# Rotation doublings by group, sample operands earlier, U copies dealt out, and output rows turned inside the last layer

## The reference

```python
h = modulate(rmsnorm(x, norm_pre[0]), sh0, sc0)
x = x + 0.5 * gt0 * rmsnorm(swiglu(h, ffn1_in, ffn1_out), norm_post[0])
h = modulate(rmsnorm(x, norm_pre[1]), sh1, sc1)
u, q, k, v, q_idx, k_idx, w_idx, gate_a, gate_b = jnp.split(h @ w_in, splits, axis=-1)
y_ssm, s_re, s_im = s5_mixer(u, h0_re, h0_im, ...)          # 32 groups of 16 channels, 64 complex states each
y_a = (y_ssm @ glu_w) * jax.nn.sigmoid(y_ssm @ glu_v)
attn = attention_fn(q, k, v, q_idx, k_idx, w_idx)           # indexer scores, top-k keys, softmax
mixed = (sigmoid(gate_a) * y_a + sigmoid(gate_b) * (attn @ w_branch_attn)) @ w_out
x = x + gt1 * rmsnorm(mixed, norm_post[1])
x = x + 0.5 * gt2 * rmsnorm(swiglu(modulate(rmsnorm(x, norm_pre[2]), sh2, sc2), ffn2_in, ffn2_out), norm_post[2])
```

## Time and profile before

| | |
|---|---|
| median of 3 runs | 3160.18 us (3159.11 to 3163.3) |
| the profiled execution, device time | 3145.66 us |
| its span (first to last instruction or transfer) | 3143.9 us |
| mean granted TensorE clock | 0.955 |
| busy: PE, DVE, ACT, POOL | 93%, 54%, 38%, 12% |
| last x block ready, first turn of the last block | 3131.74, 3132.66 us |

### The profile page before, as it was taken

How to read it: one execution, slowest core, us unless ns; L and a number is a source line. 1 busy time by engine, 2 the same in 40 slices (tenths; PEclk the granted TensorE clock), 3 DMA queues, 4 the chain that set the end, 5 groups by cost and what they waited for, 6 DMA issues and landing times. The chain is left out here.

```text
span 3143.9 us, 55982 instructions
## 1 busy us (share of the span) xinstructions
PE 2910.3 (93%) x21922; PEld 2715.4 (86%) x21922; DVE 1691.9 (54%) x3314; ACT 1191.6 (38%) x2019; POOL 379.2 (12%) x430
## 2 busy tenths in 40 slices
PE   6899999889999989999869999997999889999997
PEld 5899999789776689999848999997997766999997
DVE  5442346877768474223364424478777684732234
ACT  5532333445344243222254323344453432522221
POOL 2100000214015100000021000011240340100000
PEclk8999999899999999999979999989999999999998
DMA  7443442312123333232174434323221243232321
GB/s 241 133 150 107 135 145 78 125 48 62 48 78 109 103 105 87 77 98 83 51 234 128 147 105 145 124 77 125 55 61 50 76 128 103 83 97 84 104 73 62
DMA packets 452487, 324.09 MB, mean 103 GB/s; under 512 B 25113, under 2 KB 403345, under 8 KB 451546
## 3 DMA queue, kind: packets, MB, share of 16 engines
q1 hardware_dynamic: 446906, 296.60, 31.4%
q0 software_dynamic: 5408, 25.17, 2.4%
HBM read 310.48 MB, written 11.24 MB: 102 GB/s over the span
## 5 line engine op out<-in xcount | busy, mean ns | idle before, releaser
L1187 PE MATMUL PS<-h_hi,w_hi 128*128 128x260 f32 (+1 forms) x4000 | 840.6, 292 | 42.1 <-POOL h_lo L2678 28.3
L1187 PE MATMUL PS<-h_lo,w_hi 128*128 128x260 f32 (+1 forms) x4000 | 816.1, 286 | 0.0
L1781 DVE TENSOR_TENSOR lo_apart<-stage,w_hi 128x1024 fp32r<-128x1024 f32 (+2 forms) x448 | 498.5, 1147 | 432.8 <-ACT w_hi L779 425.8
L1187 PEld LDWEIGHTS PS<-h_hi,w_hi 128*128 128x128 f32 (+1 forms) x4000 | 629.6, 192 | 91.6 <-issue 72.9
L1187 PEld LDWEIGHTS PS<-h_lo,w_hi 128*128 128x128 f32 (+1 forms) x4000 | 627.4, 192 | 0.0
L779 ACT ACTIVATE w_hi<-stage 128x1024 fp32r<-128x1024 f32 (+3 forms) x586 | 541.8, 954 | 76.3 <-DMA stage<-in_mod_w 40.0
L1187 PE MATMUL PS<-h_hi,lo_apart 128*128 128x260 f32 x2816 | 570.3, 285 | 0.0
L1187 PEld LDWEIGHTS PS<-h_hi,lo_apart 128*128 128x128 f32 x2816 | 437.8, 190 | 0.0
L1925 DVE TENSOR_TENSOR hidf<-sil,PS 128x520 f32<-128x520 f32 x88 | 61.3, 696 | 420.9 <-PE PS L1187 420.9
L1187 PE MATMUL PS<-hid_lo,w_hi 128*128 128x260 f32 x1408 | 285.3, 284 | 0.0
L1187 PE MATMUL PS<-hid_hi,w_hi 128*128 128x260 f32 x1408 | 284.5, 283 | 0.0
(11 more groups left out here) (428 smaller groups left out, 4055.7 us busy)
## 6 DMA issues: line engine op xcount, KB each, us to landing
stage<-in_ffn_in SPq DMA_DIRECT2D x176, 512.0 KB, 3.8
stage<-in_mod_w SPq DMA_DIRECT2D x144, 512.0 KB, 4.7
stage<-in_w_in SPq DMA_DIRECT2D x72, 512.0 KB, 3.6
stage<-in_ffn_out SPq DMA_DIRECT2D x64, 384.0 KB, 3.3
stage<-in_ffn_out SPq DMA_DIRECT2D x64, 320.0 KB, 3.1
stage<-in_w_out SPq DMA_DIRECT2D x16, 512.0 KB, 3.5
x_hold<-xT SPq DMA_DIRECT2D x2, 2080.0 KB, 6.5
xT<-x_hold SPq DMA_DIRECT2D x2, 2080.0 KB, 8.2
```

The lines of the kernel that those rows point to most:

```text
L1187: return nc.tensor.matmul(out, lhsT, rhs, start=start, stop=stop)
L1781: nc.vector.tensor_tensor(lows(ch)[:, ch.slot, 0:ch.elems], stage[:, ch.slot, 0:ch.elems], w_hi[:, ch.slot, 0:ch.elems].bitcast(FP32), ALU ...
```

## The change

VectorE: all doublings leave the qi loop. Doublings 0 and 1 come after it, doubling 2 after `new_keys` in u tile 0, 3 and 4 behind score groups 1 and 3. The last two doublings are made for four pairs at a time (`last_rotations(t)`), for t = 0 before gate tile 0, for t + 1 behind `skipped(t)`. `samples_operands` stands ahead of the split of u1. The clears of BX and BXl go to GpSimd, ahead of its wait for the powers; VectorE waits for `bx_zeroed`.
ScalarE: the copies of u tile u-1 are made in quarters between the key copies of tile u; those of tile 3 stay behind it.
The end: in the last layer, TensorE turns each x block to rows as soon as it is stepped (three row tiles; the fourth for blocks 4 to 7, its blocks 0 to 3 last, because its bank holds the roots), the samples after block 2. ScalarE and VectorE copy half rows, SyncE sends each row tile when both halves are there. The rows lie over `h_hi` and `h_lo`. The block after the layers goes.

```diff
-    def chunked_inputs(u, pair):
-
-        for q in range(4):
+    def chunked_inputs(u, pair, q):
...
                 for u in range(4):
                     split(chunk('u', u + 2))
                     if u == 1:
                         keys_turned(0)
-                    for g in scored_beside(u):
+                    for n, g in enumerate(scored_beside(u)):
                         if g + 1 < PAGE // 8:
                             keys_turned(g + 1)
-                    act.wait_ge(chunk_used, chunk('u', u).number(1))
-                    for dst, src in chunked_inputs(u, (u + 1) % 2):
-                        nc.scalar.activation(dst, src, ACT.Copy)
-                    nc.scalar.activation(us[:, u, :], PS[:, (u + 1) % 2, 1, HALF - DEC:HALF], ACT.Copy).then_inc(ev_a, 1)
+                        if n < 4:
+                            inputs_by_chunk(u - 1, n)
+                for q in range(4):
+                    inputs_by_chunk(3, q)
...
+                def rows_turned_out():
+                    for k in range(KD):
+                        pe.wait_ge(x_ready, 2 * KD + k + 1)
+                        if k == 2:
+                            pe.wait_ge(xs_stepped, 3)
+                            for f in range(KD):
+                                last = turn(PS[0:DEC, 2 + f // 4, 1, f % 4 * P:(f % 4 + 1) * P], xT[:, f, T:TOK], P)
+                            last.then_inc(x_turned, 1)
+                        if k == 4:
+                            pe.wait_ge(x_copied, 1)
+                        for t in range(TT if k >= 4 else TT - 1):
+                            last = turned_row(t, k)
+                            if k == KD - 1:
+                                last.then_inc(x_turned, 1)
+                        if k == 3:
+                            last.then_inc(x_turned, 1)
+                    for k in range(4):
+                        last = turned_row(TT - 1, k)
+                    last.then_inc(x_turned, 1)
...
+                def last_rotations(t):
+                    at = slice(4 * t, 4 * t + 4)
+                    for q in (levels - 2, levels - 1):
+                        n = 1 << q
+                        x1, x2 = etmp[:, 0, :, 0:n], etmp[:, 1, :, 0:n]
+                        for r, op in enumerate((ALU.subtract, ALU.add)):
+                            cn, sn = (pw[:, 2 + q, z, at].unsqueeze(2).to_broadcast([P, 4, n]) for z in (r, 1 - r))
+                            own(nc.vector.tensor_tensor(x1, E[:, 0, at, 0:n], cn, ALU.mult))
+                            tt(x2, E[:, 1, at, 0:n], sn, ALU.mult)
+                            tt(E[:, r, at, n:2 * n], x1, x2, op)
...
                     if u == 2:
                         poles()
-                        dve.wait_ge(x_spilled, 16)
-                        own(nc.vector.memset(E[:, 0, :, 0:1], 1.0))
-                        own.step(nc.vector.memset(E[:, 1, :, 0:1], 0.0))
-                        rotations(0, 2)
-                    if u == 3:
-                        rotations(2, 5)
-                split(chunk('ki', 2))
+                dve.wait_ge(x_spilled, 16)
+                own(nc.vector.memset(E[:, 0, :, 0:1], 1.0))
+                own.step(nc.vector.memset(E[:, 1, :, 0:1], 0.0))
+                rotations(0, 2)

                 for u in range(4):
-                    split(chunk('u', u + 2))
                     if u == 0:
                         dve.wait_ge(ev_a, evicts_a['ki'] + 1)
                         samples_operands()
-                        rotations(5, 6)
+                        split(chunk('ki', 2))
                         new_keys()
+                        rotations(2, 3)
+                    split(chunk('u', u + 2))
                     for g in scored_beside(u):
                         weighted(g)
-                        if g in (0, 2):
-                            last_rotation(g // 2)
+                        if g in (1, 3):
+                            rotations(3 + g // 2, 4 + g // 2)
                         if g == 5:
                             held_inputs()
                         if g == 7:
-                            dve.wait_ge(h0_ready, 1)
-                            own(nc.vector.memset(BXl[:], 0.0))
-                            own.step(nc.vector.memset(BX[:], 0.0))
+                            dve.wait_ge(bx_zeroed, 1)
                             plain_inputs(0)
...
                 counted(0.0)
+                last_rotations(0)
...
                     if g % 4 == 3:
                         skipped(t)
+                    if g % 4 == 3 and t < 3:
+                        last_rotations(t + 1)
...
+                def half_row(t):
+                    nc.vector.tensor_copy(yrow[:, t, 512:1024], PS[:, t, 1, :]).then_inc(y_copied, 1)
+
+                if is_last:
+                    dve.wait_ge(x_turned, 4)
+                    half_row(1)
+                    dve.wait_ge(x_turned, 6)
+                    half_row(TT - 1)
...
                 pool.wait_ge(ct_ready, 2)
+                own(pool.memset(BXl[:], 0.0))
+                own.step(pool.memset(BX[:], 0.0))
+                pool.sem_inc(bx_zeroed, 1)
                 pool.wait_ge(powers_ready, 1)
```

94 lines of the change are left out of this document (53 added, 41 removed).

## The result

The changed kernel takes 3124.5 us (median; the range is 3116.7 to 3128.3) against 3160.0 us beside it; the ratio is 0.9884, with an interval of 0.9860 to 0.9908. One disturbed execution of 15567 us counts in that median (it is 3121.7 without it) and is left out of range and ratio. A second measurement gave 3122.4 against 3149.6, ratio 0.9906 (0.9888 to 0.9924). The profiled execution of after has 3118.24 us, its span is 3116.5; before it had 3145.66 and 3143.9. So the profiles are 27.4 us apart, the medians 35.5 and 27.2.

The account below looks back on a forecast made before the run. PE, busy 93%, bounds the kernel, so only its waits and low-clock stretches can pay. 39 (u stage) - 9 (doublings by group) + 4 (end) = 34 us off 3160.18, giving 3126; range 3111 to 3146.

Parts of the forecast that it names:

- The u stage: Four u tiles and sixteen page-score groups, ki's end to BX's second turns: 39 us saved over both layers, ends 38 and 41.
- the walk: New u-stage order followed instruction by instruction through the old profile: 20.7 us saved in layer 0, 17.3 in layer 1.
- The operand wait: Start of the u stage: PE waits 1.2 us for the sample operands after u0, where it waited 3.7.
- POOL is over by 591.3: Early u stage: GpSimd contention makes the sample operands at most 1.4 us a layer late; 0.3 counted.
- The wait for weighted scores: U stage: PE waits 1.0 us for group 6's scores, 2.8 before, and 0.8 for the last group's, as before.
- The "5.0 us" of the earlier start: Start of the u stage: u0 starts at 583.8 us instead of 588.8, since its split no longer follows two doublings.
- The dealt copies: U stage: ScalarE's U quarters fit between key copies, so both 2.8 us waits on ScalarE at a tile's start go.
- held by VectorE's total and not by the order: Rival, 5 in 100: half of 13 us taken off VectorE shows in the u stage; 7 us off in all, 3153.
- Doublings by group: Gate tiles: making doublings 5 and 6 for four groups at a time costs 9 us, ends 0 and 18.
- The drive waits: Gate tiles: PE's drives wait for counts, 1.5 to 2.0 us, none at layer 1's first; 9.3 in all, 5.6 stay.
- The fall of the clock that I expected in layer 0: Gate tiles, layer 0: low clock after a drive, as layer 1 had before, expected twice: 3.4 us lost.
- The end: Last x block to last DMA: 4 us saved, transfers bound by DMA rate at 400 to 445 GB/s; ends 2 and 7.

Follow-up runs that it names:

- experiment 7: Changed kernel, but GpSimd begins its first output operands only once VectorE has the sample operands ready; ratio 0.9908 to the kernel before.
- experiment 2: Changed kernel, but doublings 0 and 1 and the starting clears stand ahead of the first u chunk's split again; ratio 0.9900 to the kernel before.
- experiment 3: Changed kernel, but ScalarE copies the four quarters of a U tile together after the tile's key copies; ratio 0.9955 to the kernel before.
- experiment 1: Changed kernel, but the last two doublings are made for all groups at once again, inside the u stage; ratio 0.9943 to the kernel before.
- experiment 5: Changed kernel, but in gate tiles 3, 7 and 11 the part doublings stand behind the selection step and plain inputs; 3114.5 us, ratio 0.9885 to before.
- experiment 8: Changed kernel, but first halves of row tiles 0 to 2 are sent as soon as copied; ratio 0.9905 to the kernel before, end 80.2 us.
- experiment 9: Changed kernel, with part doublings behind selection step and plain inputs, and first halves of row tiles 0 to 2 sent early; 3108.1 us, ratio 0.9854 to before.
- experiment 6: Changed kernel, but sample operands straight behind the first u chunk's split, doublings 1 and 2 behind the new keys; ratio 0.9892 to the kernel before.
- experiment 4: Changed kernel, but output rows are turned, copied and sent in a block after the last layer, as before; ratio 0.9923 to the kernel before.

## Why the prediction was right

3126 was forecast, 3124.5 and 3122.4 came. Against the kernel before the differences are 35.5 and 27.2 us where 34 were forecast. It was right for the reasons given, in sum; in its parts there are errors that cancelled or stayed without effect, and that the sum came so near is in part luck.

**The u stage: 39 predicted, 39 measured.** Means over the seven profiles that leave the stage alone: 56.3 and 54.5 us, against 76.6 and 73.2: 20.3 + 18.7 (the walk had 20.7 + 17.3). Layer 0's second turns start 57.6 us behind ki's end, at 640.91; 640.7 was the forecast. The clock averages 0.97, the key copies release no wait. From TensorE's last ki matmul, the cleaner border, it is 20.3 + 18.2 = 38.5. The kernel before has only one profile, so its own scatter is not known.

**Its inner terms are less right.** The operand wait is 2.3 in layer 0 and not 1.2 (and nothing in layer 1). The step that was mis-sized is "POOL is over by 591.3, so the operands can be late by 1.4 us a layer at most; I count 0.3": the four copies took 1.83 us instead of 0.85, 1.0 us more, in experiment 7 shown to be GpSimd's doing. The Trainium skill (SBUF — State Buffer, Who interferes with whom) says that a VectorE copy in a two-port mode is blocked while GpSimd holds the shared ports for an instruction. The trace agrees that the copies wait, with 1.83 against 0.89 us; it does not show their mode. By that rule I had put the gain 2 us lower. Experiment 7 shows that the 1 us is worth nothing in the stage, because the next waits take it up.

The wait for weighted scores is 2.0 and 2.6 us and not 1.0, the one at the first slots 1.0 as forecast. The "5.0 us" of the earlier start is not a term of its own either: put back, it costs 3.1 and 0.2 (experiment 2). The dealt copies are worth 6 and 13 us (experiment 3), where the waits that the prediction read are 4.1 us a layer, with 2.8 us of low clock behind one in layer 0: that is near for layer 0 and too little for layer 1, where the clock fell in the experiment. And the term that the prediction put last in its story, VectorE's total, carries the most: 10 and 9 of the 11.6 us of doublings (experiment 1). I gave the rival "held by VectorE's total and not by the order" 5 in 100. Its mechanism is half true: the total does hold the stage, together with the order. What was wrong in that rival was that half of 13 us would show; of the 11.6 that experiment 1 put back, four fifths do.

**Doublings by group: 9 predicted, 8 to 10 measured.** In the gate stages it is 106.3 - 102.1 and 105.6 - 102.0 us, 4.2 + 3.6 = 7.8. The low clock behind the last drive adds 1.7 us in layer 0 and 0.1 in layer 1 (means of the same profiles), which makes 9.6. The drive waits are 8.5 us against 9.3, released by counting, all between 1.15 and 1.74. Five of the six were forecast. The sixth, layer 1's first, was put at nothing and is 1.15. The fall of the clock that I expected in layer 0 is there, behind all three of its drives; the first two rows go with the first two drives, the last row is the whole gate stage of layer 1:

```profile
675.90:681.90 6.00, 6.00 (x39) 5.98 (x39) 5.83 (x16) 0.00 (x0) 0.00 (x0) 0.72 0.00 0
705.90:711.90 6.00, 4.60 (x36) 4.39 (x35) 5.04 (x18) 4.52 (x14) 0.00 (x0) 0.89 0.34 87
...
2194.00:2310.00 116.00, 110.75 (x956) 108.88 (x957) 101.90 (x250) 55.81 (x125) 46.96 (x52) 1.00 0.23 60
```

With the stretch at 0.54 shown in experiment 5 they lose 1.7 + 0.7 + 2.8 = 5.2 us, and 1.7 more follow behind the third drive: 6.9 against the 3.4 forecast. Layer 1 of the same execution has full clock behind all three waits; the kernel before had 0.95 there. So by layer the 9 us came about otherwise than forecast. In layer 0 all waits for counts together rose only from 3.3 to 3.9 us, while TensorE's busy time in the gate stage grew by 6.0 us at the lower clock; in layer 1 they rose from 0.4 to 5.2, while its busy time fell by 4.5 at the higher. The waits' net 5.4 us are the 5.6 forecast; the clock's part was put at 3.4 in layer 0 and is 6.0 - 4.5 in these two profiles, and that is luck. In experiment 8 layer 1 has the low clock, with 108.4 us. So the waits recur, two or three in each layer of all eight profiles with this order, and the clock's part changes from one execution to the next.

**The end: 4 predicted, 3.4 measured,** and bound by the rate (experiment 8). The rate was 386 to 433 GB/s and not 400 to 445, and from the last byte to the end of the span it took some 1.6 us and not 1.0. TensorE's last eight turns took 1.09 us, the full clock, where I had allowed 0.2 us each; it made no difference, since the transfers came last anyway.

**Sum.** 39 - 7.8 + 3.4 = 34.6 us, or 32.8 with what lies behind the last drives; 34 was forecast, 35.5 and 27.2 are the differences of the medians. The profiles are 27.4 apart because later stages were 8 us longer in after's: the scoring stages 1.6 and 4.0, and 2.7 in layer 0's attention, from the last top-8 step to ScalarE's last `ex` (63.4 to 64.8 us in every other profile, 67.4 in after's). The 1.6 most likely belong to the change. The 2.7 recur in no other profile. The 4.0 are inside the scatter of the scoring stages over both layers (229.8 to 237.9), but no profile with the change has less than 232.4 in layer 1.

**Open.** Why the same waits have a low clock behind them in one execution and not in the next. What raised the clock in the unprofiled executions of experiment 9, which have 9 of its 14 us. Whether the change itself costs some us in the scoring stage of layer 1, where before had 231.5 and the twelve others 232.4 to 237.5: a second profile of before would say. And whether the 11.6 us of doublings would cost as much elsewhere in the u stage.

## What to carry to other kernels

Here one engine is fed by another that was busy 80% of a stage before the change and 90% after it. The first waits of that stage don't add: what is taken from one comes back at the next (experiments 2, 6 and 7), while 11.6 us taken from the feeding engine's total are worth 9 to 10 (experiment 1). So in such a stage move work of the feeding engine out first, even where it grows by half when it is cut into small steps for gaps elsewhere (16.8 us instead of 11.6), and put the moved steps behind whatever the fed engine waits for next (experiment 5). And compare stages between fixed borders over several profiles, not spans of two, and look whether the low clock behind the last wait of a stage falls into the next one.

## What the runs showed of the hardware

- Unchanged code of some 235 us varied by 8 us between executions, with the mean granted clock between 0.92 and 0.96. That is more than experiments 2, 4, 6, 7 and 8 moved; at most 2.9 us of it stand in the 6 us behind a drive.
- Waits of 1.28 to 1.75 us ahead of the last 16 small matmuls of a drive (32 rows, 8 columns) were followed by 6 us at a clock of 0.52 to 0.72 in 14 of 16 stages; without the wait the clock was 0.72 there in 3 of 10.
- Four 64x32 copies of VectorE took 0.85 to 0.89 us with GpSimd idle and 1.8 to 2.0 with it at work in most profiles, up to 2.55 (experiment 6). A doubling step of 32 elements took 0.18 to 0.20 once GpSimd was through, and up to 0.73 beside it.
- A TensorE wait of 5.2 us at the start of its stage cost 3.1 us, since later waits shrank, and was followed by 6 us at 0.58 (experiment 2). Key-copy waits of 4.9 and 5.5 us, two and three, came with 6.1 us at an unchanged mean clock of 0.97 and with 12.6 us at 0.90 (experiment 3).
- The end's 2 MB left at 386 to 433 GB/s in one run of transfers (mean 406), and at 367 to 435 in two (means 379 and 395).
